# Top-k search shared by VectorE and ScalarE, convolution sums in PSUM, four banks for the late projection slots

## What is computed

```python
def one_block(args):
    ...
    sc = indexer_scores(qib, wb, k_idx)
    sc = jnp.where(key_pos[None, None, :] <= q_pos[None, :, None], sc, -jnp.inf)
    _, idx = lax.top_k(sc, topk)
    return sparse_attend(qb, k[bidx, idx], v[bidx, idx], q_pos, idx, rel_table)
...
u = glu[..., :D_CONV] * jax.nn.sigmoid(glu[..., D_CONV:])
c = jax.nn.silu(layernorm(causal_dwconv(u_ext, lw['conv_dw'], lw['conv_db']), lw['conv_ln_g'], lw['conv_ln_b']))
x = x + jnp.concatenate([a, c], axis=-1) @ lw['w_o']
```

## Time and profile before

| | |
|---|---|
| median of 3 runs | 1991.23 us (1987.47 to 1996.62) |
| profiled execution | 1991.95 us |
| its span | 1990.1 us |
| busy: TensorE, VectorE | 1671.0 us (84%), 1205.3 us (61%) |
| busy: ScalarE, GpSimd | 540.6 us (27%), 550.9 us (28%) |
| mean granted TensorE clock | 0.909 of full |

### The profile page before, as it was taken

How to read it: one execution, slowest core, us unless ns; L and a number is a source line. 1 busy time by engine, 2 the same in 40 slices (tenths; PEclk the granted TensorE clock), 3 DMA queues, 4 the chain that set the end, 5 groups by cost and what they waited for, 6 DMA issues and landing times.

```text
span 1990.1 us, 28193 instructions
## 1 busy us (share of the span) xinstructions
PE 1671.0 (84%) x10229; PEld 1509.7 (76%) x10229; DVE 1205.3 (61%) x2079; ACT 540.6 (27%) x1118; POOL 550.9 (28%) x342
## 2 busy tenths in 40 slices
PE   6988999979861387799688699999999999999983
PEld 6967898873720245589678599989989989999982
DVE  5367999999999455524641845436336346336366
ACT  6345111212300365410341332203203212212212
POOL 1230432230000054323001134433433433433420
PEclk8989999985976789999885799999999999999997
DMA  7220222213620100031003011111111111111102
GB/s 231 77 55 25 71 77 78 73 30 87 183 66 20 53 11 1 1 128 42 11 17 100 22 43 48 39 46 51 43 39 48 43 43 43 43 43 43 43 15 90
DMA packets 138602, 110.60 MB, mean 56 GB/s; under 512 B 12180, under 2 KB 119948, under 8 KB 138210
## 3 DMA queue, kind: packets, MB, share of 16 engines
q1 hardware_dynamic: 128181, 102.17, 17.0%
q10 hardware_dynamic: 10301, 6.73, 1.2%
HBM read 93.54 MB, written 16.00 MB: 55 GB/s over the span
## 4 chain that ended last, share of the span: by engine, by line
PE 48%; DVE 10%; issue 4%; ACT 3%; DMA 1%; POOL 1%; DVEq 0%; ACTq 0%; SPq 0%; POOLq 0%
PE ps L1590 40%; PE ps L1605 2%; PE ps L1892 2%; PE ps L1582 2%; DVE logits L1451 1%; DVE up_conv L1534 1%; DVE n_rstd L1157 1%; DVE n_rstd L1152 1%; DVE up_conv L1533 1%; DVE logits L1448 1%; DMA out_y_prompt<-y_tok 1%; PE ps L1908 1%; PE ps L1981 1%; ACT probsT L1028 1%; DVE yT L1161 0%
## 5 line engine op out<-in xcount | busy, mean ns | idle before, releaser
L1590 PE MATMUL ps<-h_hi,w_hi 128*128 128x344 f32 x1200 | 384.5, 320 | 8.7 <-DVE xT L1552 4.7
L660 POOL TENSOR_SCALAR w_hi<-w_raw 128x1024 fp32r<-128x1024 f32 (+1 forms) x107 | 117.1, 1095 | 965.5 <-PE ps L1590 503.9
L1590 PE MATMUL ps<-h_lo,w_hi 128*128 128x344 f32 x1200 | 383.3, 319 | 0.0
L1590 PE MATMUL ps<-h_hi,w_lo 128*128 128x344 f32 x1200 | 383.2, 319 | 0.0
L662 POOL TENSOR_TENSOR w_lo<-w_raw,w_hi 128x1024 fp32r<-128x1024 f32 (+1 forms) x107 | 288.2, 2694 | 8.9
L1590 PEld LDWEIGHTS ps<-h_hi,w_hi 128*128 128x128 f32 x1200 | 225.3, 188 | 10.4 <-DVE xT L1552 5.8
L1552 DVE TENSOR_TENSOR xT<-xT,ps 128x344 f32<-128x344 f32 x264 | 135.2, 512 | 150.7 <-PE ps L1590 147.6
L1590 PEld LDWEIGHTS ps<-h_hi,w_lo 128*128 128x128 f32 x1200 | 225.6, 188 | 0.0
L1590 PEld LDWEIGHTS ps<-h_lo,w_hi 128*128 128x128 f32 x1200 | 225.4, 188 | 0.0
L1533 DVE SCALAR_TENSOR_TENSOR up_conv<-up,fw,up_conv 128x1024 f32<-128x1024 f32 x44 | 63.1, 1435 | 263.0 <-ACT upl L1107 263.0
L1590 PE MATMUL ps<-g_hi,w_hi 128*128 128x344 f32 x528 | 176.4, 334 | 36.1 <-DVE xT L1552 36.1
(11 more groups left out here) (327 smaller groups left out, 2858.8 us busy)
## 6 DMA issues: line engine op xcount, KB each, us to landing
w_raw<-in_w_up SPq DMA_DIRECT2D x44, 512.0 KB, 3.9
w_raw<-in_w_in SPq DMA_DIRECT2D x24, 512.0 KB, 4.3
w_raw<-in_w_down SPq DMA_DIRECT2D x22, 512.0 KB, 3.6
s_k_page<-in_cache_k SPq DMA_DIRECT2D x32, 256.0 KB, 2.9
s_v_pages<-in_cache_v SPq DMA_DIRECT2D x32, 256.0 KB, 2.9
xT<-x_spill SPq DMA_DIRECT2D x1, 4128.0 KB, 12.3
x_tok<-in_x_prompt SPq DMA_DIRECT2D x8, 512.0 KB, 7.1
x_spill<-x_raw SPq DMA_DIRECT2D x16, 256.0 KB, 2.7
```

The costliest lines, as they stand in the source:

```text
L660: pool.tensor_scalar(view(wh), view(wr), 1.0, 0.0, ALU.mult, ALU.add).then_inc(w_hi, 1)
L1590: mm = pe.matmul(out, view(w)[:, k, m0:m0 + m], x(k), start=(k == 0 and q == 0), stop=(k == ktiles - 1 and q == 2))
```

## The change

The counts of blocks 7 and 6 go to ScalarE, as a Sign with an accumulator (steps `top`, one behind each projection unit from the gate slots to the third k slot); VectorE counts blocks 5 to 2 and does each small step once for all six columns. A few instructions ahead of the loop compute limits for both kinds of counts, and two counts behind it settle a tie at the threshold. The transposes `ktok` and `ctok` are spread over later units. From the gate slots on a slot's units go through banks 0 to 3 in turn, and a unit waits for the copy of the one four before it. The convolution's sums go to banks 4 and 5, 512 columns an instruction, one tile after another; the sample top-k and softmax stand in the fourth tile, `sample_heads` behind the sample columns. The sample branch uses banks 6, 7, 2 and 3 instead of 4, 5 and 6, and computes the eight self scores in one batch.

```diff
+CUTS = 31
+CUT_SOFTMAX = 20
...
-    steps.append(("wsel", 0))
+    steps += [("wsel", 0), ("top", 0), ("top", 1)]
+    tops = [("top", i) for i in range(2, CUTS)]
     late = [("par", i) for i in range(4)] + [("toep", h) for h in range(NH)]
-    while pieces:
-        steps.append(pieces.pop(0))
-        if pieces and pieces[0][3] == 0 and late:
-            steps.append(late.pop(0))
-    steps += late
-    for m in range(4):
-        steps += mm(JS_K + m, KT) + [("ktok", m)]
-    for m in range(4):
-        steps += mm(JS_V + m, KT) + [("vtok", m)] + ([("ctok", 0)] if m == 1 else [])
+    for x in pieces + [x for m in range(4) for x in mm(JS_K + m, KT)] + [x for m in range(4) for x in mm(JS_V + m, KT)]:
+        steps.append(x)
+        if x[4] < KT:
+            continue
+        _, js, c, _, _ = x
+        if tops:
+            steps.append(tops.pop(0))
+        if js < JS_K:
+            if late:
+                steps.append(late.pop(0))
+        elif js < JS_V:
+            m = js - JS_K
+            steps += [("ktok", m - 1, c)] if m else []
+            steps += [("ctok", 3 * (m - 2) + c)] if m == 2 or (m, c) == (3, 0) else []
+        else:
+            m = js - JS_V
+            steps += [("ktok", 3, c)] if m == 0 else []
+            steps += [("vtok", m, i) for i in range(3)] if c == 2 else []
...
+def in_bank(js, c):
+
+    return 3 * (js % 2) + c if js < JS_GA else (UNITS_TO[js] + c - UNITS_TO[JS_GA] + 1) % 4
...
+        def count(i):
+
+            act.wait_ge(th_cand, i + 1)
+            for b in (7, 6):
+                act.activation(hits[:, HIT_AT[b]:HIT_AT[b] + IDX_EXT[b]], sc[:, IDX_AT[b]:IDX_AT[b] + IDX_EXT[b]], ACT.Sign,
+                               scale=-1.0, bias=cand[:, b - 2:b - 1], accum_out=cnt[:, b - 2:b - 1]).then_inc(th_sum, 1)
...
+        for b in (7, 6):
+            dve.tensor_scalar(col(lim, b), col(less, b), 2.0, float(IDX_EXT[b]), ALU.mult, ALU.add)
+        for b in (5, 4, 3, 2):
+            ins = dve.tensor_scalar(col(lim, b), col(less, b), -1.0, -float(IDX_EXT[b]), ALU.mult, ALU.add)
+        self_.link(ins)
+        self_.link(dve.tensor_scalar(below[:, :], lim[:, 0:4], 1.0, None, ALU.mult))
+        dve.tensor_scalar(lim[:, 0:4], lim[:, 0:4], 0.0, None, ALU.mult)
...
-        groups = ((7, 6), (5, 4, 3, 2))
-        part = lambda x, g: x[:, 4:6] if g == 0 else x[:, 0:4]
-        with dve.Fori(0, 31) as i:
-            for g in range(2):
-                dve.wait_ge(th_set, 2 * i + (g + 1))
-                dve.tensor_scalar(part(cand, g).bitcast(I32), part(th, g).bitcast(I32), bits[:, bass.ds(i, 1)], None,
-                                  ALU.bitwise_or).then_inc(th_cand, 1)
-            for g in range(2):
-                dve.wait_ge(th_cand, 2 * i + (g + 1))
-                for b in groups[g]:
-                    if b == 2:
-                        dve.wait_ge(th_cnt, 6 * i + 7)
-                    dve.tensor_scalar(hit(b), row(b), col(cand, b), col(less, b), ALU.is_ge, ALU.add,
-                                      accum_out=col(cnt, b)).then_inc(th_cnt, 1)
-            for g in range(2):
-                dve.wait_ge(th_cnt, 6 * i + (6 + (2, 6)[g]))
-                dve.scalar_tensor_tensor(out=part(keep, g), in0=part(cnt, g), scalar=0.0, in1=part(cand, g),
-                                         op0=ALU.is_ge, op1=ALU.mult).then_inc(th_keep, 1)
-            for g in range(2):
-                dve.wait_ge(th_keep, 2 * i + (g + 1))
-                dve.tensor_tensor(part(th, g), part(th, g), part(keep, g), ALU.max).then_inc(th_set, 1)
-        dve.wait_ge(th_set, 64)
-
+        with dve.Fori(0, CUTS) as i:
+            dve.wait_ge(th_set, i + 1)
+            dve.tensor_scalar(cand[:, :].bitcast(I32), th[:, :].bitcast(I32), bits[:, bass.ds(i, 1)], None, ALU.bitwise_or).then_inc(th_cand, 1)
+            dve.wait_ge(th_cand, i + 1)
+            for b in (5, 4, 3, 2):
+                if b == 2:
+                    dve.wait_ge(th_cnt, 4 * i + 7)
+                dve.tensor_scalar(hit(b), row(b), col(cand, b), col(below, b), ALU.is_lt, ALU.add,
+                                  accum_out=col(cnt, b)).then_inc(th_cnt, 1)
+            dve.wait_ge(th_cnt, 4 * i + 10)
+            dve.wait_ge(th_sum, 2 * i + 2)
+            dve.tensor_tensor(keep[:, :].bitcast(I32), cnt[:, :], lim[:, :], ALU.is_le).then_inc(th_keep, 1)
+            dve.wait_ge(th_keep, i + 1)
+            dve.scalar_tensor_tensor(out=th[:, :].bitcast(I32), in0=keep[:, :].bitcast(I32), scalar=shift[:, bass.ds(i, 1)],
+                                     in1=th[:, :].bitcast(I32), op0=ALU.logical_shift_left, op1=ALU.bitwise_or).then_inc(th_set, 1)
+        dve.wait_ge(th_set, CUTS + 1)
+
+        two = slice(4, 6)
+        self_.link(dve.scalar_tensor_tensor(out=th[:, two], in0=th[:, two], scalar=SMALLEST, in1=th[:, two], op0=ALU.is_ge, op1=ALU.mult))
+        for b in (7, 6):
+            ins = dve.tensor_scalar(hit(b), row(b), col(th, b), col(less, b), ALU.is_gt, ALU.add, accum_out=col(cnt, b))
+        self_.link(ins)
+        self_.link(dve.scalar_tensor_tensor(out=keep[:, two], in0=cnt[:, two], scalar=0.0, in1=th[:, two], op0=ALU.is_ge, op1=ALU.mult))
+        self_.link(dve.scalar_tensor_tensor(out=th[:, two], in0=keep[:, two], scalar=NEXT, in1=th[:, two], op0=ALU.mult, op1=ALU.add))
...
-        parts = (((0, 0, S), (1, 0, S)), ((2, 0, S), (3, 0, S)))
-
-        def taps(pr, j0, j1):
+        def taps(m, j0, j1):
             with dve.Fori(j0, j1) as j:
-                for e, (m, t0, n) in enumerate(parts[pr]):
-                    dve.wait_ge(tap, 2 * j + (2 * CW * pr + e - 1))
-                    dve.scalar_tensor_tensor(out=yt[e][:, 0:n], in0=u[:, m, bass.ds(j + t0, n)],
-                                             scalar=cw[:, bass.ds(CT * j + m, 1)], in1=yt[e][:, 0:n],
+                for e in range(2):
+                    dve.wait_ge(tap, 2 * j + (2 * CW * m + e - 1))
+                    dve.scalar_tensor_tensor(out=ps[:, 4 + e, :], in0=u[:, m, bass.ds(j + 512 * e, 512)],
+                                             scalar=cw[:, bass.ds(CT * j + m, 1)], in1=ps[:, 4 + e, :],
                                              op0=ALU.mult, op1=ALU.add).then_inc(tap, 1)

-        for pr in range(2):
-            for e, (m, t0, n) in enumerate(parts[pr]):
-                if pr:
-                    dve.wait_ge(tap, 2 * CW - 1 + e)
-                dve.tensor_scalar(yt[e][:, 0:n], u[:, m, HALO + t0:HALO + t0 + n], cw[:, CT * HALO + m:CT * HALO + m + 1],
+        for m in range(CT):
+            for e in range(2):
+                if m:
+                    dve.wait_ge(tap, 2 * CW * m - 1 + e)
+                dve.tensor_scalar(ps[:, 4 + e, :], u[:, m, HALO + 512 * e:HALO + 512 * (e + 1)], cw[:, CT * HALO + m:CT * HALO + m + 1],
                                   vec[:, 40 + m:41 + m], ALU.mult, ALU.add).then_inc(tap, 1)
-            between = (CUT_TOP_K, CUT_SOFTMAX)[pr]
-            taps(pr, 1, between)
-            (sample_top_k, sample_softmax)[pr]()
-            taps(pr, between, HALO)
-            for e, (m, t0, n) in enumerate(parts[pr]):
-                dve.wait_ge(tap, 2 * CW * pr + 2 * (CW - 1) - 1 + e)
-                dve.scalar_tensor_tensor(out=y[:, m, t0:t0 + n], in0=u[:, m, t0:t0 + n], scalar=cw[:, m:m + 1], in1=yt[e][:, 0:n],
-                                         op0=ALU.mult, op1=ALU.add).then_inc(tap, 1)
-        sample_heads()
+            if m < CT - 1:
+                taps(m, 1, HALO)
+            else:
+                sample_top_k()
+                taps(m, 1, CUT_SOFTMAX)
+                sample_softmax()
+                taps(m, CUT_SOFTMAX, HALO)
+            for e in range(2):
+                dve.wait_ge(tap, 2 * CW * m + 2 * (CW - 1) - 1 + e)
+                dve.scalar_tensor_tensor(out=y[:, m, 512 * e:512 * (e + 1)], in0=u[:, m, 512 * e:512 * (e + 1)], scalar=cw[:, m:m + 1],
+                                         in1=ps[:, 4 + e, :], op0=ALU.mult, op1=ALU.add).then_inc(tap, 1)
...
+        sample_heads()
...
-                if js >= 2:
+                if js >= JS_GA:
+                    pe.wait_ge(in_c, UNITS_TO[js] + c - 3)
+                elif js >= 2:
...
-            out = ps[0:cols, 3 * (js % 2) + c, 0:NM if kind == "ck" else CH]
+            out = ps[0:cols, in_bank(js, c), 0:NM if kind == "ck" else CH]
...
-            pe.matmul(ps[0:DB, 5, :], wsel[:, n, :], rsm[n % 2][:, 0:PAST], start=(n == 0), stop=(n == DB - 1))
-            pe.matmul(ps[0:DB, 6, 0:1], wsel[:, n, :], rsm[n % 2][:, PAST:KEYS], start=(n == 0), stop=(n == DB - 1)).then_inc(si_w, 1)
+            pe.matmul(ps[0:DB, 6, :], wsel[:, n, :], rsm[n % 2][:, 0:PAST], start=(n == 0), stop=(n == DB - 1))
+            if n == 0:
+                pe.wait_ge(self_r, 1)
+            pe.matmul(ps[0:DB, 7, 0:1], wsel[:, n, :], rself[:, n:n + 1], start=(n == 0), stop=(n == DB - 1)).then_inc(si_w, 1)
```

(28 more changed lines are left out.)

109 lines of the change are left out of this document (59 added, 50 removed).

## The result

The kernel after the change takes 1975.89 us, the median of 6 runs (1968.74 to 1982.84), against 1993.92 of the kernel before (6 runs, 1987.47 to 1997.7): a ratio of 0.9918, 95% interval [0.9896, 0.9940]. That is 0.8% faster, some 16 us, with an interval of 12 to 21; the forecast was 20.5 us off the profiled execution.

What follows compares the result with a forecast made beforehand. Bound seen passing from VectorE (search, convolution taps) to TensorE's late slots and the sample branch: 470.6 + 120.4 + 0.7 + 2.85 + 34.1 = 628.6, -19.0 against 647.56, -1.5 more; 1991.95 - 20.5 = 1971 us, range 1950 to 1993.

Steps and rivals of the forecast that it cites:

- The search: VectorE's top-k loop: 4.35 us an iteration, 134.9 for the loop plus 17 of stalls, ending at 354.5, 71 us earlier.
- rival (5): ScalarE's two Sign passes slower than its Exp rows; from 3.2 us they bound the iteration, at 4 us 1996; chance 0.03.
- The late slots: TensorE's projection units, held to one per search iteration: last q copy at 470.6 instead of 433.08, 37 us later.
- the part on the banks: In the late slots TensorE may run three units ahead (four banks) and two transposes while ScalarE's copies wait.
- VectorE's side: Mask 45 us, 512-column convolution taps 0.666 us each, softmax reached at 575.1, then 16.6 us waiting for the sample logits.
- rival (2): Convolution taps in PSUM at over 0.83 us: nothing gained at 0.83, 2007 us at 0.9, 2075 at 1.20; chance 0.09.
- What the PSUM sums are for: Convolution taps summing in PSUM go free of GpSimd's splits, costing VectorE 16 us; if stalled, up to 21, end 4 later.
- The LayerNorm sums' 1.5 us: First 24 matmuls took 8.77 us coming from idleness, the next 7.22; TensorE now comes straight from work, -1.5 us.
- The sum: LayerNorm sums start at 628.6 instead of 647.56, -19.0; with -1.5 more, 20.5 us off 1991.95.
- (1): ScalarE lockstep: gate-unit copies wait for GpSimd's product, counts behind them; half staying gives 1988 us, all 2004; chance 0.15.
- (3): ScalarE's Sign needs another table than Sigmoid: 24 loads of 1.283 us, +11 to +16 us, 1985; chance 0.04.
- (4): Fewer stalls and a search loop at its lower bound: loop end 12 us earlier, 1959 us; chance 0.09.

## Why the prediction was right, step by step

- **The search.** 4.43 us an iteration against 4.35, the small steps 1.25 instead of 1.17; stalls 15.1 against 17, with 8 splits in the loop against 10, and the run with the small steps in PSUM shows that GpSimd's splits and products are nearly all of them. The loop ended at 353.0; forecast 354.5 (the terms as given add up to 354.7). ScalarE's two passes took 2.26 us and are hidden; rival (5) fell.
- **The late slots.** Last q copy at 468.6 against 470.6, logits 120.6 us behind it against 120.4, sums at 627.50 against 628.6. Size and reason were right: how many units are left at the loop's end is fixed by the order of ScalarE's list. The prediction's 116.1 us from the loop's end to the last q copy came out as 115.6; with four units moved ahead they are 97.0 or 97.1 in three runs, and a shorter loop brings q earlier by as much. The prediction's own 116.6 / 27 = 4.32 us a unit makes 17.3 of those four units, and 16.7 were measured. Wrong was the part on the banks: TensorE is held by the copy of a parameter step, and a bank fewer changes nothing. On the way from q to the logits TensorE waits once for 10.7 us, put down to the load of the sample's index pages, which SP issues from 469.6 on; before it was 10.6. No run tried to load them earlier.
- **VectorE's side.** A tap took 38.27 / 58 = 0.660 against 0.666, so rival (2) fell. The choice of 0.666 over 1.20 had no row of a PSUM write behind it; that it came out is in part luck. The mask took 402.9 - 353.0 = 49.9 against 45 plus two or three stalls. VectorE waited 12.45 us for the logits against 16.6.
- **What the PSUM sums are for** is the step that failed, without touching the sum. The prediction priced them at 16 us, and taps that stall all the same at up to 21 us of VectorE's time and 4 at the end. The 16 us are there (248 x 0.660 against 124 x 1.199, 15 us), but as the price of short instructions. With the sums in SBUF it is not the taps that stall: three of GpSimd's splits take 29 to 36 us longer, and the LayerNorm sums start 71 us later (2049.06 us in the one execution timed, 1975.89 after). The share of the ports was right, who loses it was not.
- **The LayerNorm sums' 1.5 us** did not come. The first 24 products took 7.15 instead of 8.77, as forecast, but the second 24 took 8.91 instead of 7.22. The mean granted clock was 1.00 (2.4 GHz) in the first and 0.81, between the two levels, in the second; before it was 0.82 and 1.00. TensorE pauses 2.5 us between the two before and 2.8 after, so what put the low stretch here stays open.
- **The sum.** -19.0 forecast for the start of the sums, -20.06 measured. The loop's first step was 1.3 us earlier (200.60 against 201.89), where the forecast had it 0.9 later; that is luck, and without it the start would have moved by -18.8. The ratio makes 16 us and the medians 18, under the forecast's 20.5, which still lies in the interval of 12 to 21.
- **The rivals.** (1), the lockstep with GpSimd's products: one wait that fits, 2.99 us at 247.76 while GpSimd has three products to make, not the 16 it was given. With four units ahead one is named in the table of waits, 8.7 us, but it lies ahead of the first count. (3): one table load in the whole loop, so Sign and Sigmoid share a table. The Trainium skill (ScalarE: Activation LUTs, Table sets) has its cheap functions in every set without naming sign; the trace agrees if sign is one of them. (4): stalls came at 15, only 2 under the forecast, and an iteration at 4.43, over its 4.35.
- **Not tried singly:** the spread transposes, the batch of self scores and the split of the counts were never undone one by one. What each is worth stays argued from the rows.

## What to carry to other kernels

When work moves to an engine that also releases another engine's buffers, place the first of its new waits behind the releases that are ready, and then one release per wait. Six for five waits made the search 16.6 us longer here; fewer than one were not tried. Before VectorE runs a long row of instructions with two inputs in SBUF, ask what GpSimd has to do in that time; one of every two on PSUM is enough to let it in. Small serial steps that share a loop with GpSimd are worth moving to PSUM for the stalls alone.

## What was not expected of the hardware

- Instructions of VectorE with two SBUF inputs, one behind the other, keep GpSimd out for the whole row: 37.33, 30.58 and 29.91 us for an instruction of 1.05.
- A stall also hits a step with a single SBUF tensor and a column of scalars (2.36 us at L1321); with its tensor in PSUM the same step took 0.23 us beside a split.
